# Moving the places of activation tiles in SBUF in a hybrid decoder block

## The reference

```python
hs = concatenate([meta, x], axis=1)
hs = hs + 0.5 * swiglu(rmsnorm(hs, ffn1_norm), ffn1_w_gate, ffn1_w_up, ffn1_w_down)
hs = hs + token_mixing(rmsnorm(hs, mix_norm), ...)
hs = hs + 0.5 * swiglu(rmsnorm(hs, ffn2_norm), ffn2_w_gate, ffn2_w_up, ffn2_w_down)
out = rmsnorm(hs, final_norm)[:, 16:]

swiglu(h)       = (silu(h @ w_gate) * (h @ w_up)) @ w_down
token_mixing(h) : u = h @ w_in + b_in, cut into b, c, v, a, g (1024 columns each)
                  y_sc = b * causal_dwconv(c * v, 3 taps)
                  y_cf = silu(layernorm(causal_dwconv(a * sigmoid(g), 31 taps) + bias))
                  return concat(y_sc, y_cf) @ w_out
```

## Time and profile before

| | us |
|---|---|
| median of 3 runs | 1882.74 |
| the three runs | 1873.58, 1882.74, 1882.75 |
| the profiled execution, its own time | 1873.64 |
| its span, first to last instruction | 1871.8 |
| PE busy in it | 1859.9 |
| DVE busy | 1112.3 |
| ACT busy | 922.3 |

### The profile page before, as it was taken

One profiled execution on the slowest core, in us unless ns is written; L12 is line 12 of the kernel. 1 busy time (PEld: TensorE's weight loads), 2 busy tenths in 40 slices (PEclk: granted clock), 3 DMA queues, 4 the chain that ended last, 5 costly groups with the idle time before them and its releaser, 6 DMA issues.

```text
span 1871.8 us, 32101 instructions
## 1 busy us (share of the span) xinstructions
PE 1859.9 (99%) x13017; PEld 1758.7 (94%) x13017; DVE 1112.3 (59%) x1218; ACT 922.3 (49%) x1173; POOL 5.9 (0%) x17
## 2 busy tenths in 40 slices
PE   9999999999999999999999999999999999999998
PEld 9999999999999999999999999888888888888886
DVE  7555555555554545468899887555566655544444
ACT  6434333343343444359888665444444444443443
POOL 1000000000000000000000000000000000000000
PEclk9999999999999999999999999999999999999999
DMA  6655555555555555555666566666656666666664
GB/s 222 192 178 173 175 178 170 178 174 173 179 172 178 176 175 178 176 174 170 187 185 178 173 201 186 189 189 189 190 179 188 191 192 193 210 193 190 193 190 134
DMA packets 283357, 342.26 MB, mean 183 GB/s; under 512 B 10639, under 2 KB 223985, under 8 KB 283152
## 3 DMA queue, kind: packets, MB, share of 16 engines
q1 hardware_dynamic: 282672, 340.44, 58.6%
q10 hardware_dynamic: 320, 0.53, 0.1%
q0 software_dynamic: 288, 0.19, 0.0%
HBM read 339.02 MB, written 2.10 MB: 182 GB/s over the span
## 4 chain that ended last, share of the span: by engine, by line
PE 98%; DVE 1%; DMA 0%; ACT 0%; SPq 0%; issue 0%; DVEq 0%
PE ps L466 20%; PE ps L467 20%; PE ps L468 20%; PE ps L473 17%; PE ps L474 9%; PE ps L568 4%; PE ps L567 4%; PE ps L569 4%; DMA x_tok<-in_x 0%; DVE w_lo L886 0%; PE ps L428 0%; PE ps L585 0%; DVE zc L1098 0%; PE ps L591 0%; DVE ln_mu L912 0%; SPq L323 0%
## 5 line engine op out<-in xcount | busy, mean ns | idle before, releaser
L886 DVE TENSOR_TENSOR w_lo<-raw,w_hi 128x1024 fp32r<-128x1024 f32 x639 | 781.7, 1224 | 652.5 <-ACT w_hi L650 647.4
L650 ACT ACTIVATE w_hi<-raw 128x1024 fp32r<-128x1024 f32 x639 | 675.5, 1058 | 845.6 <-PE ps L468 505.6
L466 PE MATMUL ps<-x_hi,w_hi 128*128 128x272 f32 (+2 forms) x2048 | 588.1, 287 | 1.2 <-DVE x_lo L895 1.2
L467 PE MATMUL ps<-x_lo,w_hi 128*128 128x272 f32 (+2 forms) x2048 | 587.3, 287 | 0.0
L468 PE MATMUL ps<-x_hi,w_lo 128*128 128x272 f32 (+2 forms) x2048 | 583.4, 285 | 0.0
L473 PE MATMUL ps<-x_both,w_hi 128*128 128x512 f32 x1408 | 488.4, 391 | 0.0
L474 PE MATMUL ps<-x_both,w_lo 128*128 128x256 f32 x1408 | 394.1, 280 | 0.0
L467 PEld LDWEIGHTS ps<-x_lo,w_hi 128*128 128x128 f32 x2048 | 386.4, 189 | 0.1
L466 PEld LDWEIGHTS ps<-x_hi,w_hi 128*128 128x128 f32 x2048 | 384.5, 188 | 1.5 <-DVE w_lo L1120 1.4
L468 PEld LDWEIGHTS ps<-x_hi,w_lo 128*128 128x128 f32 x2048 | 385.4, 188 | 0.0
L473 PEld LDWEIGHTS ps<-x_both,w_hi 128*128 128x128 f32 x1408 | 263.3, 187 | 57.8
(11 more groups left out here) (148 smaller groups left out, 1146.5 us busy)
## 6 DMA issues: line engine op xcount, KB each, us to landing
raw<-in_ffn_w_up SPq DMA_DIRECT2D x176, 512.0 KB, 3.6
raw<-in_ffn_w_down SPq DMA_DIRECT2D x176, 512.0 KB, 4.6
raw<-in_ffn_w_gate SPq DMA_DIRECT2D x175, 512.0 KB, 3.7
raw<-in_w_in SPq DMA_DIRECT2D x80, 512.0 KB, 3.5
raw<-in_w_out SPq DMA_DIRECT2D x32, 512.0 KB, 4.7
x_tok<-in_x SPq DMA_DIRECT2D x4, 512.0 KB, 7.9
gain_tok<-in_final_norm SPq DMA_DIRECT2D x1, 1024.0 KB, 5.3
out_y<-o_tok SPq DMA_DIRECT2D x2, 512.0 KB, 2.9
```

The source lines that it names most:

```text
L466: pe.matmul(dst, w_high, act_high, start=first, stop=False)
L467: pe.matmul(dst, w_high, act_low, start=False, stop=False)
L650: act.activation(w_hi[s][:, :], raw[s][:, :], ACT.Copy).then_inc(hi_ready, 1)
L886: dve.tensor_tensor(w_lo[s][:, :], raw[s][:, :], w_hi[s][:, :].bitcast(F32), ALU.subtract).then_inc(lo_ready, 1)
```

## The change

The high and low parts of x no longer lie in two halves of the region but side by side, tile by tile, 64 bytes behind the region's start. x2 starts 64 bytes further, a2 (and a small buffer behind it) 192 bytes further, and all the buffers of the mixer 128 bytes behind the start of their region in place of 64. No instruction is added, removed or moved in any program; sizes and shapes of all operands stay.

```diff
-        x_hi = at("x_hi", x_at, [P, KD, T], F32R)
-        x_lo = at("x_lo", x_at + 4 * (KD * T + X_GAP), [P, KD, T], F32R)
-        x2_both = at("x2_both", x_at, [P, KD, 2, SEQ], F32R)
+        x_pairs = at("x_pairs", x_at + 64, [P, KD, 2, T], F32R)
+        x_hi, x_lo = x_pairs[:, :, 0, :], x_pairs[:, :, 1, :]
+        x2_both = at("x2_both", x_at + 64, [P, KD, 2, SEQ], F32R)
...
-        a2_both = at("a2_both", a_at, [P, 2, KF, SEQ], F32R)
+        a2_both = at("a2_both", a_at + 192, [P, 2, KF, SEQ], F32R)
...
-        gu2_lo = at("gu2_lo", a_at + 4 * 2 * KF * SEQ, [P, SET, SEQ])
-        assert SET * SEQ <= 2 * KF * (T - SEQ)
+        gu2_lo = at("gu2_lo", a_at + 192 + 4 * 2 * KF * SEQ, [P, SET, SEQ])
+        assert 48 + SET * SEQ <= 2 * KF * (T - SEQ)
...
-        mix_at = a_at + 64
+        mix_at = a_at + 128
```

## The result

The changed kernel is slower: 1894.26 us median of 13 runs (1888.25 to 1894.84) against 1882.74 for 13 runs of the kernel before (1871.91 to 1883.14); ratio 1.0074, 95% interval 1.0057 to 1.0092. (The ratios in this document are over all runs of both sides, so they are not the quotients of the medians, here 1.0061.) I had forecast 1870.4, faster. Its profiled execution took 1894.41 us with a span of 1892.6, against 1873.64 and 1871.8 before: 20.8 us more. The runs of both kernels fall on two levels: 1888.3 (6 runs) and 1894.5 (7) after, 1873.7 (6, one of them at 1871.9) and 1882.9 (7) before. Shorter against shorter the change costs 14.6 us, longer against longer 11.6; the two profiles compare a longer execution after with a shorter one before.

What follows compares the result with a forecast made beforehand. The prediction took PE's pace over 12,896 products as the bound. Its terms, -6.3 - 2.3 - 3.7 = -12.3 us, taken off the 1882.74 us median, gave 1870.4 us (-0.65%), range 1854 to 1884.

Steps and rivals of the forecast that it cites:

- Part 1: In `gu2`, moving x2 gives both products of a pair `out_cf`'s surplus, 11.11 ns in place of 13.33: -6.3 us.
- Part 2: In `down2`, moving a2 puts the weights relatively one place ahead, as in `out_cf`, saving 2.22 ns a product: -2.3 us.
- Part 3: In `gu1` and `ag`, x side by side gives every tile the odd tiles' 372.8 ns a triple: -3.7 us.
- Part 4: The rest: `cv` and `b` 0, within 0.8 us either way; mixer 0, between -2.8 and +1.7 us.
- The places are worth nothing: Rival for all products: the surplus is a fixed cost of switching weights, set by shapes; 1882.7 us, chance 0.13.
- The absolute place decides: Rival: the moving operand's own place counts, so `down2` gains nothing; -10.0 us, 1872.7 us, chance 0.22.
- The step decides: Rival: starting elsewhere than the last product ended is dear, so `gu1` slows; +8.5 us, 1891.2 us, chance 0.1.

Runs made afterwards that it cites:

- e2: Kernel before with only x2 moved 64 bytes and a2 (and the small buffer behind it) 192 bytes further; 1879.20 us, ratio 1.0018.
- e3: Kernel before with all weight buffers and x2 64 bytes further and the mixer buffers at 128 bytes in place of 64; 1875.32 us, one run.
- m1: TensorE alone, without the decoder block: segments of 60 products at every moving and stationary place; 512 columns with both at place 0 took 226.7 ns.
- e1: Kernel before with only x laid side by side from 64 bytes on, x2, a2 and y unmoved; 1882.47 us, ratio 1.0040.
- e9: Kernel before, unchanged, run and profiled once more; 1882.89 us, span 1881.1.
- e4: Kernel before with all mixer buffers 192 bytes behind the region's start in place of 64; 1871.01 us, one run.
- e10: Kernel before with x2 alone 32 bytes further; eight of ten runs at 1873.4 to 1873.8 us, two at 1871.8; ratio 0.9996.

## Why the prediction was wrong

**What bounds the kernel** was right: only the pace of the products changed, and in the phases whose operands moved.

**Part 1 (x2, forecast -6.3 us)** is the step that failed first: "If 11.11 holds for both of its products". It carried the surplus of a 256-column stream over to 512 columns. At distance 1 the 256-column product is indeed cheaper than at 0 (117.8 against 120.0), but the 512-column one is dearer (228.9 against 226.7). With the right price for each width a pair would cost what it did, 228.9 + 117.8 = 346.7 ns, and part 1 would have been 0. The rest is not in any single price: pairs at distance 1 take 174.4 or 176.7 a product in place of 173.3. Measured: +3.3 us in e2, +9.2 in the changed kernel's profile. The dear bound that I had written, +4.4, was too near as well.

**Part 2 (a2, -2.3)** had the relation right, as e3 and m1 show, and the sign wrong by the same step: +2.2 us.

**Part 3 (x side by side, -3.7)** summed triples as if a tile kept its cost behind another neighbour: "If their 372.8 holds for all". It held for none, 378.5 ns for even tiles and 381.5 for odd ones. The order predicted at 124.3 ns a product has two patterns, 124.8 to 124.9 and 126.7, and the decoder is on the second in both profiles of this layout (after and e1): `gu1` and `ag` +7.8 us. I had a bound of +8.5 from the dearest single step; it held, but my argument from `down1` that the step is worth 1 ns at most did not: a cost per step is not a property of the step, it belongs to the pattern of the whole stream. The rows of `down1` had said so: its order goes back at three of eight steps, and triples with the same places and the same step back take 374.9, 372.5 and 372.5 ns by their position in the block. The mean of 373.3 hid that.

**Part 4 (0)** was +0.8 for `cv` and +0.2 for `b`, 1.0 against a bound of 0.8, and +0.6 for the mixer, within its bounds. `out_cf` at 118.6 is the 256-column product at distance 2.

**The sum.** 8.8 (e1) and 5.5 (e2, by phases) and 0.6 for the mixer are 14.9 us; the shorter level of the changed kernel, 1888.3, lies 14.6 over that of the kernel before, 1873.7. The profiles differ by 6.0 more because the profile after is on its longer level: `gu2` 497.8 and not 491.8. (That the shorter level has 491.8 is taken from e2; no such execution of the changed kernel was profiled.) From longer to longer level 11.6 us are left, since there `gu2` costs 498.0 before and 497.8 after: 8.8 for x, 2.2 for a2 and 0.6 for the mixer.

**The levels.** I left the nine us between 1873.6 and 1882.7 unexplained and took the median. They are the pairs of `gu2` (e9). An unchanged kernel with TensorE busy throughout and two times 0.5% apart was a sign that a pace is not fixed by the operands, and so no sum of single costs.

**The rivals.** "The places are worth nothing" is refuted. The Trainium skill, "TensorE: Matmul & The Clock Gate", section on the steps of a matmul, has two independent read ports and hence nothing stolen from the running product. With equal shapes m1 has 226.7 to 233.3 ns by the distance between the two operands, so the trace disagrees with what follows for the pace, and the measurement decides; whether it is the ports that meet was not shown. "The absolute place decides" falls by e3 and m1. "The step decides" named the right side, but its reason is refuted: 512 columns at 1/0 go on where the last product ended, and are dearer. My range ended at 1884, at nothing gained; the loss was left at a chance of 0.09.

**Open.** Why the distance of the two starts modulo 256 bytes sets the pace was not shown; that the loading of the next stationary tile and the moving stream hinder each other in SBUF is only argued, from both being needed. That a break of the stream can change the pattern is seen in the traces (e4, e10, `gu2` after and in e2); which pattern follows it, and why executions of one kernel differ, was not shown. 15 of the 61 executions of the kernel before beside other kernels were on the longer level, 7 of 13 beside the changed kernel and 8 of 48 after that.

## What to carry to other kernels

When TensorE is the bound and its products carry a surplus over columns by clock, measure the surplus by itself, by width and by distance of the moving from the stationary start; don't carry it from one width to another. A stream of products is a pattern with memory: test a layout behind several starts, prefer one with a single pattern, and look at the pace on both sides of every break. If the same kernel has two times, compare its two traces phase by phase before predicting a change of that size.

## What the runs showed of the hardware

At a granted clock of 1.00, 2.4 GHz, with another load of stationary weights for each product, 512 columns cost 226.7 ns at distance 0, 228.9, 232.4 and 233.3 at distances of 64, 128 and 192 bytes, and 226.7 again at 512 and 768 (m1). The best of these four distances depends on the width: 0 for 512, 192 bytes for 272 (123.3 against 125.2 to 126.7) and for 256 (113.3 in three of four segments of m1, against up to 120.0). The steady paces named here are whole multiples of 6.67 ns, the time of 16 columns, over one or a few products: 34 for 512 at distance 0, 103 for three at distance 1, 17 and 18 for 256 at 3 and 0, 53 for three at 1, 89 for five at 2. And equal streams of pairs hold 173.3 or 176.7 ns a product from the second to the last of the 22 groups of `gu2`. A stop or two foreign products in the stream can change the pattern, from 174.4 to 176.7 in the changed kernel and from 176.7 to 174.4 in e2.
